# Two sums of a convolution's layer norm: four accumulated products on TensorE in place of additions on VectorE

## The reference

```
z = h @ w_in                        # h: the normed input, [512, 1024]
u = a * sigmoid(g)                  # a, g: 512 columns of z each
u = causal_depthwise_conv(u, w, b)  # 31 taps
mu = mean(u over the 512 channels);  xc = u - mu
u = silu(xc * rsqrt(mean(xc * xc) + 1e-6) * g + b)
att = forgetting_attention(q, k, v, log_f)     # 8 heads of 64
y = concatenate([u, att]) @ w_out
```

## Time and profile before

| | us |
|---|---|
| median of three runs (1890.18 to 1895.25) | 1893.68 |
| the profiled execution's own time | 1890.14 |
| its span, first to last instruction | 1888.4 |
| TensorE busy | 1791.7 (95%) |
| VectorE busy | 1085.6 (57%) |
| ScalarE busy | 441.0 (23%) |
| GpSimd busy | 1063.9 (56%) |

### The profile page before, as it was taken

The page is one execution under the profiler, slowest core; times in us unless marked ns, Lnnn a source line. Parts: engine busy times, 40 slices in busy tenths (PEclk is TensorE's granted clock), DMA queues, the critical chain, the costliest instruction groups (busy, mean ns, idle before and its releaser), DMA issues.

```text
span 1888.4 us, 22366 instructions
## 1 busy us (share of the span) xinstructions
PE 1791.7 (95%) x8270; PEld 1448.9 (77%) x8270; DVE 1085.6 (57%) x1201; ACT 441.0 (23%) x881; POOL 1063.9 (56%) x588
## 2 busy tenths in 40 slices
PE   7997888899999997999999999999999999999997
PEld 5875566678888885866888888887887788888885
DVE  7999736582534378155654352595756463526176
ACT  3213633430101123044211010121335320102011
POOL 7562363466666674641666666674444466666662
PEclk9998988999999998999999999999999999999998
DMA  6231131123333332311333333232121233333321
GB/s 218 80 99 45 46 89 45 45 89 101 96 94 100 93 97 67 112 56 34 96 93 100 91 99 100 90 101 78 56 68 56 67 93 97 101 96 94 100 90 45
DMA packets 45181, 161.32 MB, mean 85 GB/s; under 512 B 5152, under 2 KB 5664, under 8 KB 44976
## 3 DMA queue, kind: packets, MB, share of 16 engines
q1 hardware_dynamic: 43776, 157.31, 27.2%
q10 hardware_dynamic: 1328, 2.92, 0.5%
HBM read 158.11 MB, written 2.10 MB: 85 GB/s over the span
## 4 chain that ended last, share of the span: by engine, by line
PE 81%; DVE 14%; issue 2%; ACT 2%; DMA 0%; DVEq 0%; SPq 0%; ACTq 0%
PE bank L337 19%; PE bank L339 19%; PE bank L338 19%; DVE bank L1521 3%; PE bank L372 3%; PE bank L373 2%; PE bank L374 2%; DVE AL L1424 2%; PE bank L917 1%; PE bank L890 1%; DVE TMP L1703 1%; PE bank L892 1%; PE bank L891 1%; DVE X L1705 1%; PE bank L446 1%
## 5 line engine op out<-in xcount | busy, mean ns | idle before, releaser
L268 POOL TENSOR_TENSOR WL<-RAW,WH 128x1024 fp32r<-128x1024 f32 x292 | 745.6, 2554 | 24.4
L263 POOL TENSOR_SCALAR WH<-RAW 128x1024 fp32r<-128x1024 f32 x292 | 318.4, 1091 | 766.9 <-PE bank L339 381.3
L337 PE MATMUL bank<-AH,WH 128*128 128x512 f32 x848 | 331.5, 391 | 0.0
L337 PE MATMUL bank<-HH,WH 128*128 128x512 f32 x848 | 331.3, 391 | 0.0
L338 PE MATMUL bank<-HL,WH 128*128 128x512 f32 x848 | 330.1, 389 | 0.0
L339 PE MATMUL bank<-HH,WL 128*128 128x512 f32 x848 | 330.0, 389 | 0.0
L339 PE MATMUL bank<-AH,WL 128*128 128x512 f32 x848 | 330.0, 389 | 0.0
L338 PE MATMUL bank<-AL,WH 128*128 128x512 f32 x848 | 330.0, 389 | 0.0
L1733 DVE TENSOR_TENSOR HL<-TMP,HH 128x512 fp32r<-128x512 f32 x96 | 238.8, 2487 | 4.0 <-ACT HH L1216 0.8
L1211 ACT ACTIVATE TMP<-bank 128x512 f32<-128x512 f32 x96 | 57.3, 596 | 777.6 <-PE bank L339 739.0
L1739 DVE TENSOR_TENSOR Y<-Y,bank 128x512 f32<-128x512 f32 x72 | 49.5, 688 | 309.1 <-PE bank L339 309.1
(11 more groups left out here) (329 smaller groups left out, 2359.5 us busy)
## 6 DMA issues: line engine op xcount, KB each, us to landing
RAW<-wstream SPq DMA_DIRECT2D x292, 512.0 KB, 3.5
X<-xT SPq DMA_DIRECT2D x4, 512.0 KB, 7.5
out<-Y SPq DMA_DIRECT2D x8, 256.0 KB, 2.1
TMP<-memT ACTq DMA_DIRECT2D x1, 1024.0 KB, 9.2
MIX<-bands ACTq DMA_DIRECT2D x1, 768.0 KB, 6.9
BF<-masks ACTq DMA_DIRECT2D x1, 352.0 KB, 3.1
MIX<-pool_w ACTq DMA_DIRECT2D x1, 256.0 KB, 2.9
GM<-gla_masks ACTq DMA_DIRECT2D x1, 128.0 KB, 3.8
```

Of the source, the lines that this page charges most:

```text
L263: nc.gpsimd.tensor_scalar(WH[:, s, :, :].rearrange("p k n -> p (k n)"), RAW[:, s, :], 1.0, 1.0, ALU.mult, ALU.mult).then_inc(sem("w_high"), 1)
L268: nc.gpsimd.tensor_tensor(WL[:, s, :, :].rearrange("p k n -> p (k n)"), RAW[:, s, :], f32(WH[:, s, :, :].rearrange("p k n -> p (k n)")), A ...
L337: mm(bank, WH[:, slot, k, :], h(k), start=(k == 0), stop=False)
```

## The change

Each of the two sums is made on TensorE: four products with ones, one for each tile, accumulate in one PSUM bank. The first (pass 8) reads the convolution's tiles and waits for the last tap; the second reads the squares, waits for each of them, and goes to bank 6. The four additions on VectorE, their signal and the tile between them are gone. The second sum moves from pass 10 to pass 9, and with it the reciprocal root, the scaling and the gate, each one pass earlier. The fillers and the attention's own steps stay in their passes.

```diff
@@ the passes @@
-LN_SUM = (7, 9)
-LN_STAT = (8, 10)
+LN_CONV = 7
+LN_STAT = (8, 9)
...
-LN_RSQRT = 10
-LN_NORM = 10
-LN_GATE = 11
+LN_RSQRT = 9
+LN_NORM = 9
+LN_GATE = 10
...
@@ TensorE @@
                 if i == LN_STAT[0]:
-                    pe.wait_ge(sem("ln_sum"), nth("ln_sum", 1))
-                    mm(B[7][:], ONES[:], TMP[:, 3, :], start=True, stop=True).then_inc(sem("ln_stat"), 1)
+                    pe.wait_ge(sem("conv"), nth("conv", 4 * CONV_W))
+                    for c in range(4):
+                        last = mm(B[7][:], ONES[:], SG[:, c, :], start=(c == 0), stop=(c == 3))
+                    last.then_inc(sem("ln_stat"), 1)
                 if i == LN_STAT[1]:
-                    pe.wait_ge(sem("ln_sum"), nth("ln_sum", 2))
-                    mm(B[7][:], ONES[:], TMP[:, 3, :], start=True, stop=True).then_inc(sem("ln_stat"), 1)
+                    for c in range(4):
+                        pe.wait_ge(sem("ln_sq"), nth("ln_sq", c + 1))
+                        last = mm(B[6][:], ONES[:], Y[:, c, :], start=(c == 0), stop=(c == 3))
+                    last.then_inc(sem("ln_stat"), 1)
...
@@ ScalarE @@
                 if i == LN_RSQRT:
-                    rsqrt(B[7][:], B[7][:], 4 * P, "ln", ("ln_stat", 2))
+                    rsqrt(B[6][:], B[6][:], 4 * P, "ln", ("ln_stat", 2))
...
@@ VectorE @@
-                if i == LN_SUM[0]:
+                if i == LN_CONV:
                     conv(4 * CONV_W)
-                    dve.wait_ge(sem("conv"), nth("conv", 4 * CONV_W))
-                    own(v.tensor_tensor(YTAIL, SG[:, 0:2, :], SG[:, 2:4, :], ALU.add).then_inc(sem("dve_step"), 1), "dve_step")
-                    done(v.tensor_tensor(TMP[:, 3, :], YTAIL[:, 0, :], YTAIL[:, 1, :], ALU.add).then_inc(sem("ln_sum"), 1), "ln_sum")
...
-                if i == LN_SUM[1]:
-                    dve.wait_ge(sem("ln_sq"), nth("ln_sq", 4))
-                    own(v.tensor_tensor(Y[:, 0:2, :], Y[:, 0:2, :], Y[:, 2:4, :], ALU.add).then_inc(sem("dve_step"), 1), "dve_step")
-                    done(v.tensor_tensor(TMP[:, 3, :], Y[:, 0, :], Y[:, 1, :], ALU.add).then_inc(sem("ln_sum"), 1), "ln_sum")
...
                     for cc in (c, c + 1):
-                        done(v.tensor_tensor(SG[:, cc, :], SG[:, cc, :], B[7][:], ALU.mult).then_inc(sem("ln_norm"), 1), "ln_norm")
+                        done(v.tensor_tensor(SG[:, cc, :], SG[:, cc, :], B[6][:], ALU.mult).then_inc(sem("ln_norm"), 1), "ln_norm")

```

More of the change, by code:

```diff
@@ L91 @@
     "al": each(["m1", "mm", "m2", "m3", "b", "f0", "c", "f1"], "al", 8),
-    "sum": [("m1_sum", 6), ("mm_sum", 3), ("ln_sum", 2)] + each(["m2", "m3", "b", "f0", "c", "f1", "fin"], "sum", 6),
+    "sum": [("m1_sum", 6), ("mm_sum", 3)] + each(["m2", "m3", "b", "f0", "c", "f1", "fin"], "sum", 6),
     "stat": each(["m1", "m2", "m3", "b", "f0", "c", "f1", "fin"], "stat", 1),
```

## The result

The changed kernel takes 1897.43 us (median of 13 runs, 1896.07 to 1901.44), the kernel before in the same measurements 1892.04 us (13 runs). The ratio of all runs is 1.0032, 95% interval 1.0024 to 1.0039, which is 6.0 us (the two medians stand 5.4 us apart). The forecast was 1901 us, 0.4% slower, in a range from 1893 to 1905.

The account below looks back on a forecast made before the run. VectorE was taken to set the attention loop's pace, TensorE most of the rest. Last transposes 234.35 - 226.54 = 7.8 us later gave 1890.14 + 7.8 = 1897.9 profiled, median 1893.68 + 7.8 = 1901.5; forecast 1901, range 1893 to 1905.

Parts of the forecast that it names:

- The price of a sum: TensorE, each sum: four products with ones at 0.86 us take 3.44 us, adding 2.58 us to its queue.
- The root not earlier: ScalarE, second sum: reciprocal root ready at 198.16 us against 197.90 before, though its pass is one earlier.
- The loop a pass behind at the same time: VectorE after the scaling: at 200.82 us it reaches pass 10's maxima, where before these were pass 11's.
- Between 1.8 us and a whole pass, depending on GpSimd: Attention loop: the pass behind costs at least VectorE's own 1.8 us, at most a whole pass of 6.8 us.
- one debt: Attention loop: being one pass behind, with products and earlier pass counted together, ends 7.8 us later.
- What the owed pass costs: Attention loop: the pass behind, with GpSimd's splits holding VectorE, delays the last transposes from 226.54 to 234.35 us.
- the sum of 7.8 us: End of the loop: the transposes start at 234.35 instead of 226.54 us, and later stages add nothing.
- the walk's last two terms: Pass 13: a split makes it end at 225.3, 8.8 us late; passes 14 and 15: no split, transposes at 234.35.
- the clock rival: TensorE's clock falls too after stops of 1.6 to 3.4 us: +9.7 us and more, 1903.5; chance 0.11.
- the hold on the gate's first step: VectorE, pass 11: a GpSimd split holds the gate's first step until 209.7 us; the pass ends at 210.5.
- a split over a gate output and the scaling: VectorE, pass 13: a split from 220.3 to 224.2 us holds both, so the pass ends at 225.3.
- the caught-up rival: From pass 12 VectorE is spared a 1.8 us gate output and one split's hold: 0 to -3 us; chance 0.14.

Follow-up runs that it names:

- e1: Changed kernel's four products per sum on TensorE, but every stage of the norm in the pass it had in the kernel before; 1895.93 us, ratio 1.0028.
- e4: Changed kernel with one product in place of four in each sum and the norm's old passes, timing only; 1890.52 us, ratio 0.9992.
- e2: Kernel before, additions kept on VectorE, with second sum, root, scaling and gate one pass earlier; 1894.69 us, ratio 1.0023.
- e5: Changed kernel with the loop's four GpSimd weight splits cut from 1024 to 64 columns, timing only; 1889.10 us, ratio 0.9988.
- e6: Kernel before with the loop's four GpSimd weight splits cut to 64 columns, timing only; 1887.42 us, ratio 0.9978.
- e7: Changed kernel with six more unread products with ones filling two TensorE stops, to keep its clock up; 1896.29 us, ratio 1.0030.
- e8: Kernel before with the second product right behind pass 10's scores and the root right behind the exponentials; 1890.52 us, ratio 0.9998.

## Why the prediction was right, and where its parts were not

- **The price of a sum** (3.44 us from rows of 0.86): measured 3.44. e1 against e4 shows 5.1 of the 5.2 us at T, so with the products in place this is the larger part of the loss (5.3 us in e1, 2.3 more with the pass); in e2, without them, the pass alone costs 5.0.
- **The root not earlier**: forecast 198.16; the part ahead of the change ran 0.6 us ahead (181.40 against 181.99), and it came at 197.52, within 0.05 us of the forecast. The stop was 6.32 us for 6.4.
- **The loop a pass behind at the same time**: as written, maxima of pass 10 at 200.36 (200.82 less 0.46).
- **"Between 1.8 us and a whole pass, depending on GpSimd"**: e5 and e6 give 4.2 us without the splits and without a fall of the clock, where the forecast had 1.8 as the least. That the rest is the round of scores, maxima, exponentials and transposes between the engines is likely, but no run isolates it.
- The share of the products and of the pass: the forecast let both run into one debt. The table tells them apart: 5.2 us of TensorE's products that reach T in full; a pass that lengthens T - S by 7.3 us and brings the root 2.3 us forward (e2, with additions), or by 6.7 and 4.4 us (with four products).
- **What the owed pass costs**: the sum of 7.8 us was met by 7.6 from the convolution's end, 7.0 in the trace and 6 in the runs, but not by the walk's last two terms. One sum has a small slip: the clock rival's 9.7 us give 1903.4, not 1903.5.

VectorE's timeline of the changed kernel in passes 11 to 14:

```profile
208.59 2.56 DVE L1670 TENSOR_SCALAR TMP<-TMP,SUMI 128x384 f32<-128x384 f32 x1
...
212.51 2.84 DVE L1640 TENSOR_TENSOR MIX<-MIX,Y 128x512 f32<-128x512 f32 x1
...
224.19 1.02 DVE L1657 TENSOR_REDUCE MAXI<-bank 128x1 f32<-128x384 f32 x2 [3.01 <-PE bank L583]
```

And GpSimd's:

```profile
208.54 2.39 POOL L268 TENSOR_TENSOR WL<-RAW,WH 128x1024 fp32r<-128x1024 f32 x1
...
212.13 2.67 POOL L268 TENSOR_TENSOR WL<-RAW,WH 128x1024 fp32r<-128x1024 f32 x1
221.12 1.04 POOL L263 TENSOR_SCALAR WH<-RAW 128x1024 fp32r<-128x1024 f32 x1 [6.32 <-PE bank L527]
```

In passes 11 and 12 the splits came late and one behind the other (208.54, 212.13) and held one of the scalings of step 10's probabilities for 2.56 us and the gate output for 2.84. That is about as much as the forecast had, though in pass 11 it had put the hold on the gate's first step. In pass 13 it had put a split over a gate output and the scaling, from 220.3 to 224.2. Measured, the split came at 221.12, just as VectorE ended both and stopped for the scores, for 3.01 us: that is the caught-up rival's mechanism. In its place stood the clock rival's. At 0.50 TensorE took from 217.28 to 222.91, where pass 14's scores start, for the work of pass 13. In the kernel before this took from 210.07 to 213.25, 2.4 us less:

```profile
210.07 0.63 PE L567 MATMUL bank<-IDENT,Y 128*128 128x128 f32 x4 [2.27 <-DVE Y L1673]
...
213.25 0.92 PE L580 MATMUL bank<-MIX 64*128 64x384 f32 x4
```

So a hold that was forecast was missing, and the slow clock of a rival with a chance of only 0.11 was there. That the sum of 7.8 us came out all the same is in this part luck. The two aren't independent either: e7 shows that with a faster clock the splits come earlier and hold VectorE again.

What stays open: how much the falls of the clock cost. e7 moved one and gained 0.9 us at T; e1 and e4 each have one that the kernel before has not, and their T - S is 0.7 us longer; and in e5 and e6 the falls went together with the splits.

## What to carry to other kernels

Before a step of a chain is moved a pass earlier in an in-order loop, compare what the pass holds back on each engine with how much earlier its input is ready: here the input had to be some 7 us earlier (4 with short splits), and in the changed kernel it was no earlier at all. An operation "off the busy engine" is priced where it lands: 3.8 us of additions that partly lay beside other work became 5.2 us on TensorE, which has no idle time between the first sum and the root. And before shortening a wait, look for the next fixed event behind it: in e8 a split at a set time swallowed a gain of 1.7 us whole.

## What was not expected of the hardware

The granted clock of TensorE fell to 0.50 after a stop of 3.81 us, and to 0.76 on average over 4 us after one of 1.76, while the kernel before kept 1.00 through a stop of 3.14 us. In e1 the stop at the same step, 3.13 us long, was followed by 0.53 on average from 206 to 213 us. And ahead of the change, where both kernels do the same, TensorE stops for 2.54 us before 172.98 in one trace and for 2.53 us before 172.75 in the other. The kernel before then has 0.50 from 174.5 to 176 us, the changed one full clock:

```profile
174.50:176.00 1.50, 1.50 (x20) 1.09 (x20) 1.50 (x3) 0.70 (x2) 0.00 (x0) 1.00 0.38 147
```

So in these traces the length of a stop alone did not decide whether the clock fell.
